# The causal mask of each step's own block: added by VectorE in PSUM instead of by a TensorE matmul

## What is computed

```python
def block(i):
    start = i * Q_BLOCK
    qb = lax.dynamic_slice_in_dim(q, start, Q_BLOCK, axis=2)
    s = jnp.einsum('bhqd,bhkd->bhqk', qb, k) * scale
    s = s + cb[..., :, None] - c[..., None, :]
    qpos = start + jnp.arange(Q_BLOCK)
    s = jnp.where(kpos[None, :] <= qpos[:, None], s, neg)
    p = jax.nn.softmax(s, axis=-1)
    return jnp.einsum('bhqk,bhkd->bhqd', p, v)
```

## Time and profile before

| | us |
|---|---|
| median of 3 runs | 1206.43 (1206.03 to 1206.48) |
| the profiled execution, its own time | 1207.46 |
| the span of its instructions | 1205.7 |
| PE busy | 1166.5 (97%) |
| DVE busy | 665.0 (55%) |
| ACT busy | 516.3 (43%) |
| POOL busy | 555.3 (46%) |

### The profile page before, as it was taken

The page is one execution under the profiler, slowest core; times in us unless marked ns, Lnnn a source line. Parts: engine busy times, 40 slices in busy tenths (PEclk is TensorE's granted clock), DMA queues, the critical chain, the costliest instruction groups (busy, mean ns, idle before and its releaser), DMA issues.

```text
span 1205.7 us, 17301 instructions
## 1 busy us (share of the span) xinstructions
PE 1166.5 (97%) x5816; PEld 953.8 (79%) x5816; DVE 665.0 (55%) x1005; ACT 516.3 (43%) x839; POOL 555.3 (46%) x342
## 2 busy tenths in 40 slices
PE   5999999999999999899999999999999999988998
PEld 3888888888888887688787887878878878777887
DVE  7544323323324335757768677586776766866541
ACT  6311111111111212375665755757567466575510
POOL 6232322232233544457465575664665746555410
PEclk9999999999999999999999999999999999989999
DMA  6111111111111222111010100101001101002142
GB/s 209 36 53 53 52 52 35 52 52 52 35 52 70 90 86 71 35 45 36 19 36 20 35 19 16 40 31 36 18 17 35 35 18 35 18 18 70 55 159 84
DMA packets 19408, 59.76 MB, mean 50 GB/s; under 512 B 3760, under 2 KB 3760, under 8 KB 19376
## 3 DMA queue, kind: packets, MB, share of 16 engines
q1 hardware_dynamic: 19232, 59.34, 14.8%
q10 hardware_dynamic: 144, 0.00, 0.0%
HBM read 50.68 MB, written 8.65 MB: 49 GB/s over the span
## 4 chain that ended last, share of the span: by engine, by line
PE 82%; DVE 9%; issue 4%; ACT 3%; DMA 1%; POOL 0%; ACTq 0%; DVEq 0%; SPq 0%
PE ps L390 65%; PE ps L510 6%; PE ps L491 5%; PE ps L470 4%; DVE neg_max L1114 2%; DVE newton L1169 2%; DVE h_lo L978 1%; DVE newton L1165 1%; DVE newton L1167 1%; PE ps L533 1%; PE ps L474 1%; DMA x_t<-in_x 1%; DVE pt_lo L1128 1%; ACT p_small L792 0%; ACT y L906 0%
## 5 line engine op out<-in xcount | busy, mean ns | idle before, releaser
L390 PE MATMUL ps<-h_hi,w_hi 128*128 128x512 f32 x1160 | 474.9, 409 | 19.9 <-DVE h_lo L978 13.6
L390 PE MATMUL ps<-h_hi,w_lo 128*128 128x512 f32 x1160 | 455.6, 393 | 0.0
L390 PE MATMUL ps<-h_lo,w_hi 128*128 128x512 f32 x1160 | 454.0, 391 | 0.0
L1328 POOL TENSOR_TENSOR w_lo<-w_raw,w_hi 128x1024 fp32r<-128x1024 f32 x81 | 200.1, 2471 | 290.2 <-ACT w_hi L680 290.0
L390 PEld LDWEIGHTS ps<-h_hi,w_hi 128*128 128x128 f32 x1160 | 220.0, 190 | 61.1 <-DVE h_lo L978 9.3
L390 PEld LDWEIGHTS ps<-h_hi,w_lo 128*128 128x128 f32 x1160 | 218.5, 188 | 47.4
L390 PEld LDWEIGHTS ps<-h_lo,w_hi 128*128 128x128 f32 x1160 | 219.8, 189 | 35.3 <-issue 0.5
L680 ACT ACTIVATE w_hi<-w_raw 128x1024 fp32r<-128x1024 f32 x81 | 85.6, 1057 | 258.8 <-PE ps L390 256.9
L1375 POOL TENSOR_TENSOR p_big<-p_big,rdenom 128x896 f32<-128x896 f32 (+1 forms) x64 | 94.5, 1477 | 87.4 <-DVE rdenom L1122 86.8
L1114 DVE TENSOR_REDUCE neg_max<-ps 128x1 f32<-128x896 f32 (+7 forms) x128 | 96.4, 753 | 61.5 <-PE ps L474 61.0
L1128 DVE TENSOR_TENSOR pt_lo<-ps,pt_hi 128x512 fp32r<-128x512 f32 (+1 forms) x160 | 97.4, 633 | 55.4 <-ACT pt_hi L802 53.1
(11 more groups left out here) (134 smaller groups left out, 1456.7 us busy)
## 6 DMA issues: line engine op xcount, KB each, us to landing
w_raw<-in_w_cin SPq DMA_DIRECT2D x32, 512.0 KB, 3.3
w_raw<-in_w_ain SPq DMA_DIRECT2D x32, 512.0 KB, 3.3
x_t<-in_x SPq DMA_DIRECT2D x8, 512.0 KB, 9.0
w_raw<-in_w_cout SPq DMA_DIRECT2D x8, 512.0 KB, 3.3
x_dram<-x_t SPq DMA_DIRECT2D x8, 512.0 KB, 2.6
w_raw<-in_w_aout SPq DMA_DIRECT2D x8, 512.0 KB, 3.8
out<-y SPq DMA_DIRECT2D x7, 512.0 KB, 7.1
qn<-x_dram SPq DMA_DIRECT2D x4, 512.0 KB, 3.5
```

Of the source, the lines that this page charges most:

```text
L390: last = mm(ps[:, bank, :], st[:, slot, k, :], mov[:, k, halves(h)], start=(k == 0 and st is w_hi and mov is mov_hi), stop=(k == end and s ...
L1328: TT(w_lo[:, slot, :, :], w_raw[:, slot, :, :], w_hi[:, slot, :, :].bitcast(F32), ALU.subtract).then_inc(s_wlo, 1)
```

## The change

PE no longer issues the mask matmul of line 474; the last score matmul now closes the accumulation and signals `s_sc`. On DVE, `row_max` gets one operation ahead of the reduction: a tensor_tensor add of 128 x 128, in place in PSUM, of the step's own block and the bf16 mask. It signals a new semaphore `s_mk`, and the reduction waits for that.

```diff
@@ PE: scores @@
                     last_c = c == n - 1
                     for a, b in ((q1, k1), (q2, k2)):
                         last = mm(ps[:, bank, 0:w], a[:, side, qs:qs + P],
-                                  b[:, side, c * w:(c + 1) * w],
-                                  start=(a is q1), stop=(a is q2 and not last_c))
-                    if last_c:
-                        last = mm(ps[:, bank, w - P:w], ident_bf[:, :], mask_bf[:, 0:P],
-                                  start=False, stop=True)
+                                  b[:, side, c * w:(c + 1) * w], start=(a is q1), stop=(a is q2))
                 last.then_inc(s_sc, 1)
@@ DVE: row_max @@
                 dve.wait_ge(s_sc, 16 * pair + 2 * i + par + 1)
+                bank, end = (B_SCORE + 1, w // 2) if t >= 2 else (B_SCORE + par, w)
+                own_block = ps[:, bank, end - P:end]
+                TT(own_block, own_block, mask_bf[:, 0:P], ALU.add).then_inc(s_mk, 1)
+                dve.wait_ge(s_mk, 16 * pair + 2 * i + par + 1)
```

More of the change, by code:

```diff
@@ L204, in hybrid @@
         s_sc = sem("scores_done")
+        s_mk = sem("scores_masked")
         s_max = sem("row_max_done")
```

## The result

The changed kernel takes **1210.33 us** (median of 7 runs, 1209.65 to 1211.26); before, measured beside it, takes 1206.43 (median of 7, 1206.03 to 1208.79). The ratio is 1.003, 95% interval 1.0018 to 1.0042: slower by 3.9 us. 1209.6 was predicted. The profiled execution took 1210.93 us in place of 1207.46, its span 1209.1 in place of 1205.7.

The account below looks back on a forecast made before the run. A trip bound by PE on one stretch and by a chain through ACT and DVE on the other; seven trips of +0.42 us are 2.9, trip 1 adds 0.2, trip 8 about 0: +3.1, 1209.6 us, range 1203 to 1215.5.

Parts of the forecast that it names:

- a mask lies on one kind of ground, the add on the other: In a trip, PE bounds one stretch, where masks cost it 0.12 us; ACT and DVE bound some 20 of 78 us.
- Step 1: From the pv of (5,1) to the head square of kernel step 2: nine masks less two waits, shift -0.62 us.
- Step 2: From the head square of kernel step 2 to the exp of (3,1): two adds +0.64 us, 0.49 absorbed, shift -0.47.
- Step 3: From the exp of (3,1) to the pv of (5,1): adds of (4,0), (4,1), (5,0) add 0.89 us, to +0.42.
- the four adds: In trip 8, adds before the maxima of (0,0), (0,1), (1,0), (2,0) lie on the chain: 1.21 us.
- the ten masks: In trip 8 behind 1101 us, removed masks give 1.1 us back, less 0.15 for a waiting transpose.
- contention: POOL's SBUF work slows DVE's add to 0.45 us; 0.65 more a trip, 1214 us; chance 0.05.
- PE's saving wins: PE's shorter work outweighs the adds; up to 14.7 us won, 1191.7 us, half of it 1199; chance 0.18.
- The clock drops more often: Longer PE waits at step 5 cost two to six further trips 1.56 us each; 1212.7 to 1219 us; chance 0.22.

Follow-up runs that it names:

- e10: Against before: DVE adds the mask only at (2,0), PE's matmul elsewhere; a trip takes 77.84 us, 0.11 less (one run, 1205.80 us).
- e9: Against before: DVE adds the mask only at (4,0), PE's matmul elsewhere; a trip takes 78.30 us, +0.35 (one run, 1209.80 us).
- e1: Against the changed kernel: PE's mask matmul is kept in (3,0), (3,1), (4,0), (4,1), (5,0), DVE adds in the other 11 halves; 1203.77 us.
- e2: Against the changed kernel: DVE adds only in (3,0), (3,1), (4,0), (4,1), (5,0), PE's mask matmul in the other 11 halves; 1214.34 us.
- e7: Against before: DVE adds the mask only at (3,0) and (3,1), PE's matmul elsewhere; a trip takes 77.88 us (one run, 1205.22 us).
- e12: Against the changed kernel: in half (5,0) of trip 8 alone the mask stays a matmul on PE; 1209.57 us.
- e4: Against the changed kernel: no mask at all, neither PE's matmul nor DVE's add; 1195.88 us.
- e11: Against the changed kernel: DVE adds only at (0,0), (1,0), (1,1), (2,0), (2,1), (3,0), (6,0), (6,1) of trips 1 to 7, PE's matmul elsewhere; 1199.86 us.
- e3: Against the changed kernel: PE's mask matmul is kept in all halves and DVE adds a tile of zeros; 1220.89 us.
- e5: Against the changed kernel: DVE adds only at (0,0), (1,0), (1,1), (2,0), (2,1), (6,1) of trips 1 to 7, PE's matmul elsewhere; 1200.81 us.
- e6: Against the changed kernel: trip 8 goes back to PE's mask matmul, trips 1 to 7 keep the whole change; 1209.62 us.
- e8: Against before: DVE adds the mask only at (7,0) and (7,1), PE's matmul elsewhere; a trip takes 77.86 us (one run, 1206.61 us).

## Why the prediction was right, and where its steps were not

**The unit prices.** A mask matmul was taken at 0.12 us; e10 has 0.11. The add was taken at 0.28 + 0.04 where DVE is behind; it takes 0.292, and e9's one add costs 0.35. The reading "a mask lies on one kind of ground, the add on the other" is shown by e1 and e2, and most plainly by e9 and e10.

**Step 1, -0.62, came out at -0.32.** It named two waits in PE's ground and there are three. At (7,1), the scores and the product of pt_lo with v, first before, then after:

```profile
752.51 0.40 PE L470 MATMUL ps<-k,q 128*128 128x256 f32 x2
...
752.99 0.28 PE L510 MATMUL ps<-pt_lo,v_st 128*128 128x256 f32 x1
```

```profile
753.43 0.40 PE L471 MATMUL ps<-k,q 128*128 128x256 f32 x2
...
754.04 0.28 PE L507 MATMUL ps<-pt_lo,v_st 128*128 128x256 f32 x1
```

Before, that product begins 0.48 us behind the scores, with the mask and a product of pt_hi between; by the mask's 0.12 it should now be 0.36, and it is 0.61: a wait of 0.25 us, where 0.27 was predicted.

At (1,0), the scores before, and after with the matmul in front of them:

```profile
687.79 0.74 PE L470 MATMUL ps<-k,q 128*128 128x320 f32 x4
```

```profile
688.22 0.39 PE L391 MATMUL ps<-h_hi,w_lo 128*128 128x512 f32 x1
688.56 0.85 PE L471 MATMUL ps<-k,q 128*128 128x320 f32 x4
```

ACT's reading of the sum of (0,1), 687.32 in the earlier trace rows, began 0.47 us ahead of the scores; in after it begins at 688.32, 0.24 ahead. The scores follow the matmul in front of them after 0.34 us, 0.11 more than the usual 0.23, and take 0.11 more than before: 0.22 us, where 0.16 was estimated.

The third wait, at the boundary, 0.19 us, was missed. The question "what stands behind the new instruction on its engine, and who waits for that?" was asked of pt_lo and of the exp, and not of q's split at the end of the trip, whose 0.94 us to spare looked ample. So nine masks give 8 x 0.11 + 0.07 = 0.95 by e10 and e7, the three waits take 0.25 + 0.22 + 0.19 = 0.66, and 0.29 is left, where the points above show 0.32.

**Step 2, from -0.62 to -0.47, went the other way.** It charged DVE with two adds (0.64) and let the exp of (3,1) absorb 0.49. In truth the exp follows ACT's two guesses, and these follow PE's head square of step 3, which is still PE's ground: two more masks, of (2,1) and (3,0), brought it from -0.32 to -0.53, and the exp has the same shift, -0.52. The adds cost nothing there: the row maximum of (3,1) comes nearer to the exp, but still ends at 714.83 us, 0.13 ahead of it (before, 0.53). e7 shows it alone: both adds of step 3 are made, and the trip is 0.07 shorter. The step failed by treating "DVE works without a pause" as "DVE is on the chain".

**Step 3, +0.89, came out at +0.91** (from -0.52 to +0.39). e2 has 0.87 a trip with the same three adds, which agrees.

The misses of steps 1 and 2, +0.30 and -0.35 in the change that each makes, nearly cancel. That the sum of a trip, 0.42 against 0.39, is so close is luck; that step 3 holds is not.

**Trips and ends.** From the start of attention to the pv of (5,1) of trip 7 the kernel loses 2.84 us (the difference goes from -0.22 to +2.62), where the prediction had 3.1. In it trip 1, up to its own pv of (5,1), was to cost 0.2 more than the others and cost 0.4 more (0.74). From there to the scores of (7,1) of trip 8 it loses another 0.99, where the prediction had about 0: the largest miss of all its terms. Up to the scores of (3,0) trip 8 is 0.77 us longer, nearer to the four adds that were counted there. Behind them the ten masks were to give 0.95 back, and 0.41 are lost instead. Most of that is the meeting at step 5, 1.08 us by after and e12. The prediction had named the mechanism under contention, with the row of 2.77 us, and had ruled it out for the new operation only: the add itself doesn't contend, but it shifts one that does. e12 shows this.

**The rivals.** PE's saving wins: no, though e4 puts the most that was to be had at 10.5 us, not 14.7. Without five of the adds it is what happens (e1). The clock drops more often: no. Before and after have one each in trips 1 to 7, both at the same place of a trip. After, the stretch with the wait at step 5 and the one behind it:

```profile
809.90:813.30 3.40, 1.92 (x8) 0.94 (x6) 3.19 (x7) 2.00 (x5) 1.53 (x2) 1.00 0.00 0
813.30:816.70 3.40, 3.25 (x12) 2.96 (x13) 2.37 (x5) 2.20 (x4) 0.56 (x1) 0.50 0.00 0
```

PE was busy for 1.92 us of 3.40 and then ran at half clock, 1.2 GHz, as in the earlier trace rows with 2.17 of 3.42. That trip took 79.77 in place of 78.36 us, 1.4 more. PE's three waits at step 5 add up to 1.62 us or more in every trip of after, and to 1.22 to 1.29 in before (the prediction had some 0.3 us more, it is 0.4), and still only one trip fell. Contention on the add itself: no, 292 ns mean over 128.

## What to carry to other kernels

Moving an operation from a busy engine to an idle one is not one trade but one for every place where it stands: the gain is there only where the first engine bounds, the cost only where the second does. Here one add on the wrong stretch costs three times what a mask gives on the right one. So price it for each place, along the chain in order of time, and move only those that lie right; the busy shares were the same in both cases. Ask also of every operation that the new one delays whether it meets another engine at a shared resource, and give it the same look as the new operation itself.

## What was unexpected of the hardware

- A matmul that waits on a semaphore needs its producer to be done well ahead. At the boundary 0.43 us between DVE's end and the scores already cost 0.1 us ahead of them and 0.1 in them; 0.57 to 0.61 (e11) and 0.94 (before) cost nothing.
- An operation of 0.67 us becomes 2.65 if it starts 0.29 us behind POOL's, and stays at 0.67 if it starts 0.05 ahead of it. In e3 0.05 us behind was enough for 2.89. A shift of 0.3 us decides over 1 us of PE's waiting.
- Clock drops in trips 1 to 7 came in no profile of e4, e5, e7, e10, e11 and e12, once in those of before, after, e1, e2, e6, e8 and e9, and twice in that of e3. All began 55 to 57 us into a trip, behind the waits of step 5. After, e6 and e12 are the same program up to trip 8 and have one, one and none, so the count differs between executions of one program. What picks the trip I can't say.
